# First operands of the output projection made under the last merge unit, and another order at the head of the feed-forward

## What is computed

```python
    merged = jax.nn.sigmoid(gate_a) * y_a + jax.nn.sigmoid(gate_b) * y_b
    return merged @ w_out
...
    return (jax.nn.silu(hn @ w_gate) * (hn @ w_up)) @ w_down
...
        h = h + hybrid_mixer(rms_norm(h, norm_mix_w[l]), ...)
        h = h + swiglu_ffn(rms_norm(h, norm_ffn_w[l]), w_ffn_gate[l], w_ffn_up[l], w_ffn_down[l])
```

## Time and profile before

| what | us |
|---|---|
| median of 3 runs | 2781.86 |
| lowest and highest | 2781.43, 2783.2 |
| the profiled execution | 2782.89 |
| its span, first to last instruction | 2781.1 |
| PE busy | 2694.5 (97%) |
| DVE busy | 1837.8 (66%) |
| ACT busy | 998.6 (36%) |
| mean granted clock of PE | 0.988 |

### The profile page before, as it was taken

How to read it: one execution, slowest core, us unless ns; L and a number is a source line. 1 busy time by engine, 2 the same in 40 slices (tenths; PEclk the granted TensorE clock), 3 DMA queues, 4 the chain that set the end, 5 groups by cost and what they waited for, 6 DMA issues and landing times.

```text
span 2781.1 us, 44509 instructions
## 1 busy us (share of the span) xinstructions
PE 2694.5 (97%) x17640; PEld 2451.1 (88%) x17640; DVE 1837.8 (66%) x1766; ACT 998.6 (36%) x1025; POOL 357.4 (13%) x356
## 2 busy tenths in 40 slices
PE   8999999999999999988979999999999998999997
PEld 7999988888889977867869999999999997788885
DVE  4444555555553234448888888888788887888886
ACT  4433322222222232213344444444444443333333
POOL 5000144444442500110030000000000000000000
PEclk9999999999999999999989999999999999999998
DMA  4333222222223324677434444544445449656661
GB/s 142 91 90 90 77 76 77 82 76 82 75 83 91 106 83 162 233 263 261 138 121 148 143 147 145 171 153 152 148 154 169 147 132 306 232 189 211 214 210 61
DMA packets 345652, 398.70 MB, mean 143 GB/s; under 512 B 11481, under 2 KB 300386, under 8 KB 344418
## 3 DMA queue, kind: packets, MB, share of 16 engines
q1 hardware_dynamic: 286514, 334.34, 37.5%
q10 hardware_dynamic: 59072, 63.44, 6.6%
HBM read 325.92 MB, written 71.83 MB: 143 GB/s over the span
## 4 chain that ended last, share of the span: by engine, by line
PE 92%; DVE 3%; issue 2%; DMA 1%; POOL 1%; ACT 1%; SPq 0%; DVEq 0%; ACTq 0%; POOLq 0%
PE psum L1869 33%; PE psum L2181 10%; PE psum L2180 10%; PE psum L2179 10%; PE psum L2156 6%; PE psum L2157 6%; PE psum L2158 6%; PE psum L2029 2%; PE psum L2024 1%; PE psum L1819 1%; PE psum L1847 1%; DMA w_raw<-in_w_proj_a 1%; PE psum L2008 1%; DVE hq L1657 1%; PE psum L2101 0%
## 5 line engine op out<-in xcount | busy, mean ns | idle before, releaser
L1869 PE MATMUL psum<-hn_lo,w_hi 128*128 128x264 f32 (+1 forms) x1600 | 453.5, 332 | 0.0
L1869 PE MATMUL psum<-hn_hi,w_lo 128*128 128x264 f32 (+1 forms) x1600 | 453.4, 332 | 0.0
L1869 PE MATMUL psum<-hn_hi,w_hi 128*128 128x264 f32 (+1 forms) x1600 | 452.8, 332 | 0.0
L1235 DVE TENSOR_TENSOR w_lo<-w_raw,w_hi 128x1024 fp32r<-128x1024 f32 x176 | 227.2, 1292 | 330.9 <-ACT w_hi L866 330.4
L866 ACT ACTIVATE w_hi<-w_raw 128x1024 fp32r<-128x1024 f32 x176 | 185.1, 1056 | 452.4 <-PE psum L1869 397.5
L1869 PEld LDWEIGHTS psum<-hn_hi,w_hi 128*128 128x128 f32 x1600 | 270.4, 189 | 23.0 <-issue 0.2
L1869 PEld LDWEIGHTS psum<-hn_lo,w_hi 128*128 128x128 f32 x1600 | 269.5, 188 | 23.9 <-issue 0.7
L1869 PEld LDWEIGHTS psum<-hn_hi,w_lo 128*128 128x128 f32 x1600 | 269.8, 189 | 23.2
L2156 PE MATMUL psum<-dn_hi,act_hl 128*128 128x512 f32 x616 | 244.6, 397 | 14.0 <-DVE hq L1657 12.9
L2157 PE MATMUL psum<-dn_lo,act_hl 128*128 128x512 f32 x616 | 244.0, 396 | 0.0
L2158 PE MATMUL psum<-dn_hi,act_hl 128*128 128x512 f32 x616 | 243.0, 395 | 0.0
(11 more groups left out here) (350 smaller groups left out, 6276.9 us busy)
## 6 DMA issues: line engine op xcount, KB each, us to landing
w_raw<-in_w_in SPq DMA_DIRECT2D x144, 512.0 KB, 3.6
ffn_raw<-in_w_ffn_gate SPq DMA_DIRECT2D x44, 1024.0 KB, 6.5
ffn_raw<-in_w_ffn_up SPq DMA_DIRECT2D x44, 1024.0 KB, 6.5
dn_raw<-in_w_ffn_down SPq DMA_DIRECT2D x40, 1024.0 KB, 7.2
act_hl<-act_dram SPq DMA_DIRECT2D x70, 512.0 KB, 9.0
act_dram<-comb_hi ACTq DMA_DIRECT2D x22, 896.0 KB, 4.2
act_dram<-comb_lo ACTq DMA_DIRECT2D x22, 896.0 KB, 6.3
out_raw<-in_w_out SPq DMA_DIRECT2D x16, 1024.0 KB, 10.0
```

The source lines that it names most:

```text
L1235: dve.tensor_tensor(wlo[s][:], raw[s][:], whi[s][:].bitcast(F32), ALU.subtract).then_inc(S["lo_ready"], 1)
L1869: ins = pe.matmul(o, lhs, r, start=kt == 0 and i == 0, stop=kt == 4 * n_chunks - 1 and i == 2)
```

## The change

Three things are done. (1) Of the first unit of the output projection the splits of b11, b21 and t2, the sums t1, t3 and t2 and the low halves of b11, b21 and t2 move from behind the last merge unit into it. (2) In the first unit of the feed-forward ACT makes all four weight splits before the pieces of y, DVE makes `low_2`, `low_b` and `low_c` earlier (the last one lies over `ident`, so `ident` is copied into two diagonals first), the sum S2 goes into the buffer of S4, the sum S4 is made later, POOL's two pieces of A22 become one DVE operation, and the next unit's weights are split after all of this unit's own work. (3) `rows_dve` is divided into `rows_begin` and the rest; for the down projection the order stays. PE's and SP's programs keep their order.

```diff
-                low_pieces(4 * i, 4 + 2 * i)
+                low_pieces(4 * i, 4)
...
+            def merge_act(u, splits=True):
+                for c in range(4):
+                    if c == 3:
+                        if not splits:
+                            rows_split(OUT, 0, "b11")
+                            rows_split(OUT, 0, "b21")
+                            rows_split(OUT, 0, "t2")
+                        act.wait_ge(S["mg_sum"], 4 * u + 4)
...
             for m in range(OUT_UNITS):
                 for q, what in enumerate(OUT.order(m)):
-                    rows_split(OUT, m, what)
+                    if m > 0 or q > 2:
+                        rows_split(OUT, m, what)
...
             split_a(0, 0)
+            split_2(0)
+            split_b(0)
+            split_c(0, 0)
             for n, (c, t, kh) in enumerate(A_PIECES[0:4]):
...
-            split_2(0)
-            split_b(0)
-            for n, c in enumerate((S1, S2)):
-                act.wait_ge(S["s_sum"], n + 1)
-                act.activation(s_hi[c][:], s_sum[c][:], ACT.Copy).then_inc(S["x_hi"], 1)
...
+            def first_unit_act():
+
+                evict_p1(0, 0)
+                s_high(S1, s_sum[S1][:], 1)
+                s_high(S2, s_sum[S4][:], 2)
+                s_high(S3, s_sum[S3][:], 3)
+                for c, t, kh in A_PIECES[4:6]:
+                    act.activation(s_piece(s_hi, c, t), y_piece(t, kh), ACT.Copy).then_inc(S["x_hi"], 1)
+                evict_u2(0, 0)
+                s_high(S4, s_sum[S4][:], 4)
+                evict_q5(0, 0)
+                split_a(0, 1)
+                split_2(1)
+                split_b(1)
...
+            def rows_begin(st):
 
                 rows_sum(st, 0, "t1")
                 rows_sum(st, 0, "t3")
+                rows_low(st, 0, "b11")
+                rows_sum(st, 0, "t2")
+                rows_low(st, 0, "b21")
+
+            def rows_dve(st, beside=lambda m, q: None):
+
                 for m in range(st.units()):
                     for q, what in enumerate(st.order(m)):
+                        if m == 0 and q < (3 if st is OUT else 2):
+                            continue
...
+                    if c == 3:
+                        if not splits:
+                            rows_begin(OUT)
+                        for m in range(2):
...
+                        if not splits:
+                            rows_low(OUT, 0, "t2")
+                        dve.wait_ge(S["merged_sum"], FREE["merged_sum"] + 2 * u + 2)
...
+            for t in range(2, TT):
+                dve.tensor_copy(diag[TT + 1 + t][:], ident[:]).then_inc(S["vectors_more"], 1)
...
             low_a(0, 0)
+            low_2(0)
+            low_b(0)
             rows_read(OUT, last, 6)
+            low_c(0, 0)
...
+            s_low(S2, s2_sum[:], 6)
+            s_low(S1, s_sum[S1][:], 5)
+            c_11(0, 0)
...
+            dve.tensor_tensor(by_tile(s_sum[S4]), by_tile(s2_sum), y_half(0, 1), ALU.add).then_inc(S["s_sum"], 1)
+            s_low(S3, s_sum[S3][:], 7)
...
+            s_low(S4, s_sum[S4][:], 10)
+            dve.wait_ge(S["x_hi"], X0 + 9)
+            dve.tensor_tensor(by_tile(s_lo[A22]), y_half(1, 1), by_tile(s_hi[A22]).bitcast(F32), ALU.subtract) \
+                .then_inc(S["x_lo_v"], 1)
...
-                      S4: ("x_lo_v", 4), A22: ("x_lo", 6)}
+                      S4: ("x_lo_v", 4), A22: ("x_lo_v", 5)}
```

More of the change, by code:

```diff
@@ L839, in low_pieces @@
                     c, t, kh = A_PIECES[n]
-                    pool.wait_ge(S["x_hi"], X0 + (n + 1 if c != A22 else n + 3))
+                    pool.wait_ge(S["x_hi"], X0 + n + 1)
                     pool.tensor_tensor(s_piece(s_lo, c, t), y_piece(t, kh), s_piece(s_hi, c, t).bitcast(F32), ALU.subtract) \
@@ L1177, in beside @@
                         comb_high(j - 1)
-                unit_act(j, 0, False, beside)
+                if first:
+                    first_unit_act()
+                else:
+                    unit_act(j, 0, False, beside)
                 if not first:
@@ L1521, in _, with rows_sum @@
             z_unit(N_Z - 1, zb_tiles)
+            def rows_sum(st, m, what):
+                k, (t1, t3) = st.kappa[m // 2], (b[:, 0:st.kappa[m // 2], :] for b in rows_buffers(st)[3:5])
+                b11, b12, b21, b22 = (rows_block(st, m, i) for i in range(4))
+                w11, w12, w21, w22 = (b[0][:, 0:k, :] for b in (b11, b12, b21, b22))
+                if what == "t1":
+                    if m > 0:
+                        dve.wait_ge(S["lo_ready"], st.group + st.count(m - 1, "t4"))
+                    elif st is DN:
+                        dve.wait_ge(S["chunk_used"], USED0 + 7 * (UNITS - 1) + 3)
+                    dve.wait_ge(b11[1], b11[2])
+                    dve.wait_ge(b12[1], b12[2])
+                    ins = dve.tensor_tensor(t1, w11, w12, ALU.add)
+                elif what == "t3":
+                    if m > 0:
+                        dve.wait_ge(S["lo_ready"], st.group + st.count(m - 1, "t3"))
+                    elif st is DN:
+                        dve.wait_ge(S["chunk_used"], USED0 + 7 * (UNITS - 1) + 4)
+                    dve.wait_ge(b22[1], b22[2])
+                    ins = dve.tensor_tensor(t3, w12, w22, ALU.add)
+                elif what == "t2":
+                    dve.wait_ge(S["dn_t"], st.sums + 4 * m + 2)
+                    ins = dve.tensor_tensor(w12, t1, w22, ALU.add)
+                else:
+                    dve.wait_ge(b21[1], b21[2])
+                    dve.wait_ge(S["dn_t"], st.sums + 4 * m + 3)
+                    dve.wait_ge(S["lo_ready"], st.group + st.count(m, "t1"))
+                    ins = dve.tensor_tensor(t1, w12, w21, ALU.add)
+                ins.then_inc(S["dn_t"], 1)
@@ new lines, in rows_begin @@
+            def rows_begin(st):
+                rows_sum(st, 0, "t1")
+                rows_sum(st, 0, "t3")
+                rows_low(st, 0, "b11")
+                rows_sum(st, 0, "t2")
+                rows_low(st, 0, "b21")
+            def rows_dve(st, beside=lambda m, q: None):
+                for m in range(st.units()):
+                    for q, what in enumerate(st.order(m)):
+                        if m == 0 and q < (3 if st is OUT else 2):
+                            continue
+                        if m > 0 and q == 0:
+                            rows_sum(st, m, "t1")
+                            rows_sum(st, m, "t3")
+                        if what == "b21":
+                            rows_sum(st, m, "t2")
+                        x = 7 * m + q
+                        if x >= 3:
+                            rows_read(st, (x - 3) // 7, (x - 3) % 7)
+                        rows_low(st, m, what)
+                        if q == 3:
+                            rows_sum(st, m, "t4")
+                        beside(m, q)
@@ L1660, in rows_dve @@
-            def rows_dve(st, beside=lambda m, q: None):
-                rows_sum(st, 0, "t1")
-                rows_sum(st, 0, "t3")
-                for m in range(st.units()):
-                    for q, what in enumerate(st.order(m)):
-                        if m > 0 and q == 0:
-                            rows_sum(st, m, "t1")
-                            rows_sum(st, m, "t3")
-                        if what == "b21":
-                            rows_sum(st, m, "t2")
-                        x = 7 * m + q
-                        if x >= 3:
-                            rows_read(st, (x - 3) // 7, (x - 3) % 7)
-                        rows_low(st, m, what)
-                        if q == 3:
-                            rows_sum(st, m, "t4")
-                        beside(m, q)
@@ L1784, in beside_down @@
             def beside_down(m, q):
-                if m == 0 and q == 1:
-                    up_products(PAIRS - 1)
                 if m == 0 and q == 3:
                     comb_low(PAIRS - 1)
+            rows_begin(DN)
+            up_products(PAIRS - 1)
             rows_dve(DN, beside_down)
```

173 lines of the change are left out of this document (75 added, 98 removed).

## The result

The changed kernel takes 2791.55 us (median of 6 runs, 2789.89 to 2793.65), the one before 2781.86 in the same comparison: a ratio of 1.0034, 95% interval 1.0024 to 1.0045. The forecast was 2787.2 with a range up to 2791.0: slower, which is right, but by 5.3 us and not 9.7, with the larger chance on "within 0.2%" and the time 0.55 us outside the range. The profiled execution of the changed kernel took 2789.89 us (span 2787.8) and was the fastest of its six; the one before took 2782.89 (span 2781.1).

A forecast was written before the change was run, and what follows sets the result against it. PE was taken as busy nearly all the time, so only its stalls could be won. A 0.3 us gain at the merge and 5.6 us lost in the feed-forward made +5.3 on 2781.9: 2787.2 us, range 2779.5 to 2791.

The forecast's parts named there:

- Part 1: Output projection's first operands made under the last merge unit: net gain 0.3 us, bounds 2.8 gained and 0.6 lost.
- does not move: Next unit's b22 load, in SP's program behind the last merge store's wait, lands at 1288.8 regardless; t4 2.8 us earlier.
- The clock term of this part: At t4 in the output projection, PE's idle time of some 15 us brings back the lower clock, costing 2.5 us.
- Part 2: Feed-forward's first unit reordered: unit 1 starts later, costing 5.6 us, bounds 2.6 and 8.8.
- From W to S2: Feed-forward's first unit: product S2 starts 9.3 us behind W, the end of weighing, where it was 16.9 before.
- From W to A22: Feed-forward's first unit: A22 starts 27.0 us behind W, the end of weighing, after a new 3.9 us stall.
- up to 1.6 of low clock behind it; I take 0.9: At A22 in the feed-forward's first unit, the lower clock behind the new stall costs 0.9 us, at most 1.6.
- The rule on the shared lock: Feed-forward's head: two-input DVE operations and POOL's pieces exclude each other; taken in turns, A11 starts 2.3 us later.
- the other reading: Feed-forward's head: DVE keeps the lock, A11 starts at 1432.5, weighing ends about 1446; total changes by under 1 us.
- Rival 1: Before the output projection, the first stall simply goes, every operand being ready under the merge: 2765.6 us; chance 0.05.
- Rival 2: Feed-forward's head: DVE and POOL hardly meet, weighing still ends at 1437.6: 2776.6 to 2779.1 us; chance 0.15.
- Rival 3: At the merge, t2's low half runs into POOL's merge sum and holds it: 2788 to 2791 us; chance 0.07.

The follow-up runs named there:

- e2: Kernel before with only the feed-forward part of the change, the merge and output projection as before; 2789.71 us against 2782.69 before.
- e1: Kernel before with only the merge part of the change, the feed-forward as before; 2782.85 us against 2782.69 before.
- e10: Kernel before with a mixed feed-forward first unit: old order up to the weighing's end plus t2's low half, tail much as changed; 2779.56 us against 2782.60 before.
- e5: The changed kernel itself, measured again in a later batch; 2791.76 us against 2782.41 for the kernel before.
- e9: Changed kernel with the last read of the output projection ahead of lo_b on VectorE; 2790.76 us against 2782.60 for the kernel before.
- e12: Changed kernel with extra unused matmuls ahead of the waits of t4, S2 and A22; 2785.61 us against 2782.39 for the kernel before.
- e3: e1 with VectorE's sums t1, t3 and t2 of the output projection's unit 1 moved behind reads or low halves; 2774.00 us against 2782.69 before.
- e4: e3 with SyncE issuing unit 1's four residual loads behind its loads of b21 and b22; 2767.57 us against 2782.69 before.

## Why the prediction was wrong

**Part 1, merge.** The mechanism was right in each step: b11 at once, t2 3.7 us late behind DVE's read, and t4 not before the load of the next unit's b22. That t4 started at 1292.37 where 1292.3 was predicted is luck, since this execution ended its merge 1.2 us earlier. The step that failed is the load that "does not move" and the 2.8 us gained by it. Counted from the end of the merge, t4 starts at 53.7 us (1292.37 - 1238.67) against 55.2 before (1295.08 - 1239.91), so 1.5 us are gained: the load was issued 1.1 us sooner and took 2.2 us longer. That is no chance of one execution. The same load in e2, which has the merge of before:

```profile
L525 SPq DMA_DIRECT2D out_raw<-in_w_out x1: 2921/2921/2921, 1272.8 to 1272.8; - x1
...
DMA to landing us min/median/max: 14.3/14.3/14.3
```

And in e1, which has the changed one:

```profile
L525 SPq DMA_DIRECT2D out_raw<-in_w_out x1: 4209/4209/4209, 1273.9 to 1273.9; - x1
...
DMA to landing us min/median/max: 16.4/16.4/16.4
```

In the three profiles with the old order at the merge (before, e2, e10) b22 lands 48.3 to 48.9 us behind the merge's end, in the eight with the merge part and the old place of the sum t3 (changed, e1, e5 to e9, e12) 49.9 to 50.7. The loads ahead of it are the same and in the same order (nine behind the wait for the merge stores, where the prediction counts seven); why it lands later stays open.

The clock term of this part held. 2.5 us were put down as lost behind t4's wait; 4.6 us at 0.50 make t4's product 2.1 us longer in the changed kernel, 5.4 us at 0.50 lose 2.7 in e1. The half clock behind t2's wait costs nothing here, as PE then waits over 13 us ahead of t4 anyway. Predicted was -0.3 for the part. In e1 it is 1.3 gained (t4 at 53.9 us) less 2.7 lost, so +1.4, which is its M and lies past the bound of 0.6; its median says +0.2.

**Part 2, the head.** Idle before A11: 3.7 predicted, 3.50 measured. From A11 to W: 18.2 predicted, 17.5 in the first profile and 18.4 in e5's. Counted from the merge's end W comes 8.8 us later than before (206.4 against 197.7), as predicted. From W to S2: 9.3, and 9.33. From W to A22: 27.0, and 27.0 in the first profile; 28.1 in e5's, whose w_up load took 9.1 us where I had 7.8. All of that held. As was said, the shorter stream behind W gave back what the late weighing took. The failed term is the last, "up to 1.6 of low clock behind it; I take 0.9": A22 took 5.3 us where 3.7 stood in the sum, so the clock lost 2.55 and not 0.9, past the 1.6 that it was held to cost at most; in e5 A22 took 4.75 us, which is 2.0 lost. The 1.6 is half of 3.2 us at 0.50, the stretch that the earlier trace rows shows behind an idle time of 3.1 us; the stall here is 4.86 us where 3.9 was predicted, as S4's product was done 0.9 us sooner, and the half clock covers the product from its first matmul to its last. Why it lasts longer here than in the earlier trace rows no run shows. The part costs 7.3 us by M and F in e2 (7.0 by the median), where 5.6 was predicted.

**Sum and range.** By profiles, unit 1 of the feed-forward starts 7.2 us later after the merge's end than before (238.7 against 231.5), and 9.1 us in e5; 5.3 was forecast. In the first profile the way from 5.3 to 7.2 is 0.9 of part 1 (1.5 gained less 2.1 lost, where a gain of 0.3 stood) and 1.65 behind A22's stall, less 0.7 by which W followed A11 sooner. In e5 it is 1.5 of part 1, 1.1 behind A22's stall, 1.1 of a longer w_up load and small terms. My bounds (0.6 and 8.8) add up to 9.4, which is what was measured, while the stated range ended at 2791.0, below that sum. That they fit is luck, since part 1 by M went past its bound and part 2 stayed within.

**The rule on the shared lock.** DVE's `lo_a`, `lo_2`, `lo_b` took 2.64, 3.41 and 4.42 us, where 2.29, 1.2 and 2.29 are their lengths alone, and POOL's four pieces took 14.46: the two engines went in turns. In this trace that answers what the Trainium skill ("SBUF — State Buffer", section "Who interferes with whom") leaves open about the exclusive lock: here the waiting engine got it, although DVE's next operation followed at once. The prediction holds that the other reading would change the total by under 1 us; no run shows that. e9 shows that moving one operation merely decides which of DVE's next meets POOL.

**Rivals.** Rival 1 (the first stall simply goes) was priced at 2765.6 and said to need the load 15 us earlier. e3 and e4 show a cheaper way to most of it that I had not seen: leave the waits for the stores and change the order, DVE's around the reads and SyncE's around the four loads of h. Rival 2 fell (W came 7.5 us late on the clock of the trace). Rival 3 fell too: the low half of t2 ended at 1243.4, ahead of POOL's merge sum at 1244.60, which its store released.

## What to carry to other kernels

When work is pulled ahead of a stall, follow the stream of the engine that frees the next bank. Here a read queued behind a sum that needs a late load turned a wait of 19.4 us into waits of 18.8, and the merge part gained nothing; with the sum moved behind the reads it gained 8.7 us, and with four loads issued later 15.1. Price a new wait of TensorE at both levels of the clock, for the whole product behind it: in the changed kernel the half clock cost nothing behind t2's wait, as a longer wait followed, 2.1 us behind t4's and 2.55 behind A22's. And don't take the landing of a load as fixed because its own instructions haven't moved. Leave two-input work of VectorE out of a stretch in which GpSimd has its own, save for what fits in a hole.
